# Filling the causal latent attention with projection products of later stages, and normalising one step ahead

## The reference, cut to what matters

```python
c_q = rms_norm(q_down, q_norm_g)                       # (512, 384)
q = (c_q @ w_uq).reshape(B, S, 8, 128 + 64)            # 8 heads
q_nope, q_rope = q[..., :128], apply_rope(q[..., 128:], cos, sin)
c_kv = rms_norm(kv_down, kv_norm_g)                    # (512, 256)
k_nope = (c_kv @ w_uk).reshape(B, S, 8, 128)
v = (c_kv @ w_uv).reshape(B, S, 8, 128)
# for each block i of 128 queries, each head h:
s = (q_nope @ k_nope.T + q_rope @ k_rope.T) * 192 ** -0.5
s = where(key <= query, s, -1e30)
o = softmax(s) @ v
```

## Time and profile before

| | |
|---|---|
| median of 3 runs | 1750.23 us (1749.51 to 1750.47) |
| the profiled execution | 1749.98 us, of which the span is 1748.1 us |
| PE busy | 1664.5 us, 95% |
| DVE, ACT, POOL busy | 859.7 us (49%), 580.7 us (33%), 536.2 us (31%) |
| mean granted PE clock | 0.978 of full |
| first scores of the first half | at 919.6 us |
| first half's last output done | at 962.25 us |
| second half's first scores | at 988.3 us |
| end of its last output, first `pool` tile begins | at 1030.8 us |
| third `pool` tile begins | at 1042.0 us |

### The profile page before, as it was taken

One profiled execution on the slowest core, in us unless ns is written; L12 is line 12 of the kernel. 1 busy time (PEld: TensorE's weight loads), 2 busy tenths in 40 slices (PEclk: granted clock), 3 DMA queues, 4 the chain that ended last, 5 costly groups with the idle time before them and its releaser, 6 DMA issues. The chain is left out here.

```text
span 1748.1 us, 20572 instructions
## 1 busy us (share of the span) xinstructions
PE 1664.5 (95%) x7732; PEld 1251.1 (72%) x7732; DVE 859.7 (49%) x1437; ACT 580.7 (33%) x956; POOL 536.2 (31%) x225
## 2 busy tenths in 40 slices
PE   6999889999999999999998899999999979999996
PEld 4878668887888888887775668888777855556553
DVE  4338476125644466335676854352334454334335
ACT  4117454334322244334424232342343231211113
POOL 3432126732344446732421214464324200000000
PEclk9999999999999999999999999999999989999998
DMA  4321113522322323521221112243313359888871
GB/s 163 97 84 49 61 62 121 168 85 67 95 89 94 97 86 124 165 85 37 85 73 37 60 49 92 92 143 98 95 48 97 152 182 371 331 341 337 334 289 49
DMA packets 50195, 226.51 MB, mean 130 GB/s; under 512 B 5952, under 2 KB 6848, under 8 KB 45504
## 3 DMA queue, kind: packets, MB, share of 16 engines
q1 hardware_dynamic: 48384, 220.50, 36.4%
q10 hardware_dynamic: 1728, 4.87, 0.8%
HBM read 223.25 MB, written 2.10 MB: 129 GB/s over the span
## 5 line engine op out<-in xcount | busy, mean ns | idle before, releaser
L488 POOL TENSOR_TENSOR lo_ring<-w_ring,hi_ring 128x1024 fp32r<-128x1024 f32 x219 | 535.7, 2447 | 852.3 <-ACT hi_ring L507 852.0
L507 ACT ACTIVATE hi_ring<-w_ring 128x1024 fp32r<-128x1024 f32 x219 | 231.4, 1059 | 657.0 <-PE G L1630 656.6
L1630 PE MATMUL G<-xa_hi,hi_ring 128*128 128x512 f32 x928 | 379.8, 409 | 19.5 <-POOL lo_ring L488 12.5
L1630 PE MATMUL G<-xa_hi,lo_ring 128*128 128x512 f32 x928 | 372.6, 402 | 0.0
L1630 PE MATMUL G<-xa_lo,hi_ring 128*128 128x512 f32 x928 | 370.0, 399 | 0.0
L1630 PEld LDWEIGHTS G<-xa_hi,hi_ring 128*128 128x128 f32 x928 | 176.8, 191 | 64.4 <-issue 14.1
L1630 PEld LDWEIGHTS G<-xa_lo,hi_ring 128*128 128x128 f32 x928 | 177.1, 191 | 44.6 <-issue 1.7
L1630 PEld LDWEIGHTS G<-xa_hi,lo_ring 128*128 128x128 f32 x928 | 176.7, 190 | 41.9
L1630 PE MATMUL G<-yb_hi,hi_ring 128*128 128x512 f32 x388 | 154.6, 398 | 0.0
L1630 PE MATMUL G<-yb_lo,hi_ring 128*128 128x512 f32 x388 | 151.8, 391 | 0.0
L1630 PE MATMUL G<-yb_hi,lo_ring 128*128 128x512 f32 x388 | 151.6, 391 | 0.0
(11 more groups left out here) (298 smaller groups left out, 2629.6 us busy)
## 6 DMA issues: line engine op xcount, KB each, us to landing
w_ring<-in_stream_dram SPq DMA_DIRECT2D x219, 512.0 KB, 3.6
arena<-in_w_gu_dram SPq DMA_DIRECT2D x16, 2048.0 KB, 8.1
ex_rings<-in_w_dn_dram SPq DMA_DIRECT2D x40, 512.0 KB, 13.6
ex_low<-in_w_gu_dram SPq DMA_DIRECT2D x8, 2048.0 KB, 12.5
ex_rings<-in_w_gu_dram SPq DMA_DIRECT2D x8, 2048.0 KB, 12.4
arena<-in_w_dn_dram SPq DMA_DIRECT2D x16, 512.0 KB, 11.5
sq<-in_w_dn_dram SPq DMA_DIRECT2D x8, 512.0 KB, 15.4
X<-in_x_in_dram SPq DMA_DIRECT2D x8, 256.0 KB, 6.2
```

What stands on the lines that cost most here:

```text
L488: nc.gpsimd.tensor_tensor(lo_ring[:, s, :], w_ring[:, s, :], hi_ring[:, s, :], ALU.subtract).then_inc(low, 1)
L507: nc.scalar.activation(hi_ring[:, m % RING, :], w_ring[:, m % RING, :], ACT.Copy).then_inc(high, 1)
L1630: return nc.tensor.matmul(*args, **kw)
```

## The change

In the first half, only `uv0`, `uk0` and `uq0` are made ahead of the steps. The products of `uv1` and `uk1` are cut into 16 pieces of three matmuls and PE does one piece in each step (two ahead of the first step, none in the last two). In the second half, the 16 pieces are those of the first two `pool` tiles. The pieces write banks 2 and 1 of `G` in turn, so the scores move from banks 2 and 3 to banks 3 and 0. The values and keys of the second half get places of their own, `vh1` and `kn1`, which lie over the parts of `yb_hi` and `yb_lo` that the same heads' outputs fill later. DVE takes the pieces' banks out in its odd steps (`beside`), normalises one step ahead, and scales `X` in the second half's steps. ACT rounds two of the next weight units after its first three exponentials and one more in step 10. PE's waits for the queries of steps 2 and 3 go up by one.

```diff
@@ -340,6 +340,8 @@
         vh = A(6016, 4, T)
         mP, mPT = A(8064, 2, T), A(9088, 4, T)
         qn, kn = U[:, 0:4, :], U[:, 4:8, :]
+        vh1 = ex_raw[:, 2:4, :].rearrange("p a b -> p (a b)").rearrange("p (h c) -> p h c", h=4)
+        kn1 = ex_low[:, 4 * T:KT * T].rearrange("p (h c) -> p h c", h=4)
         b_gl, b_gs, b_tmp = A(8064, 2, T), A(9088, 2, T), A(10112, T)
         pu, pa, pb_ = A(0, T + 16), A(528, T + 16), A(1056, T + 16)
         edge = A(1600, 4, 16)
@@ -387,7 +389,10 @@
             return u % 4
 
         def score(u, lo, hi):
-            first = ACC0["e_ag"] + u // TT if u < SU["x0"] else 3 if u >= SU["x2"] else 0
+            if u < SU["x0"]:
+                first = ACC0["e_ag"] + u // TT
+            else:
+                first = 3 if u >= SU["x2"] else 1 if u >= SU["mla"] else 0
             return S[:, at(u), lo:hi] if at(u) < 2 else G[:, (first + at(u)) % BANKS, lo:hi]
 
         def prob(probs, u, lo, hi):
@@ -404,6 +409,9 @@
 
         def x2_o(j):
             return (O[:, :], G[:, 0, :], TR[:, :], O[:, :])[j]
+
+        def beside_bank(n):
+            return 2 - n % 2
 
         block = ctx.enter_context(nc.Block())
 
@@ -701,29 +709,34 @@
                 unit_done("qd", j)
                 norm_tile("qd", j, U[:, j, :], V("q_norm", j), lat_hi[:, j, :], (evac, ACC0["qd"] + j + 1))
             base = SU["mla"]
+            unit_done("uv0", 0)
+            norm_root("qd", 384)
+            unit_done("uk0", 0)
             for half in range(2):
-                for name, k in ((f"uv{half}", 1), (f"uk{half}", 1), (f"uq{half}", 3)):
-                    for j in range(k):
-                        unit_done(name, j)
-                        if name == "uv0":
-                            norm_root("qd", 384)
+                unit_done(f"uq{half}", 0)
 
                 def one(u):
                     exps(base + u, 1, P * (u % TT + 1), 192 ** -0.5, mP)
 
                 for u in range(3):
                     one(16 * half + u)
+                for j in range(1, 3):
+                    unit_done(f"uq{half}", j)
                 for u in range(16 * half, 16 * half + 16):
                     t = u % TT
                     copy_t(base + u, mPT[:, 0:t + 1, t * P:(t + 1) * P], P * (t + 1), True)
                     if u + 3 < 16 * half + 16:
                         one(u + 3)
+                    if u % 16 == 10:
+                        unit_done("pool" if half else "uv1", 0)
                     if t == TT - 1:
                         j = u // TT
                         high_of((o_full, OB["mla"] + j + 1), O[:, :], yb_hi[:, j, :])
+                if half == 0:
+                    unit_done("uk1", 0)
             act.dma_start(edge, pool_edge).then_inc(edge_land, 16)
             act.dma_start(m2raw, mem2_in).then_inc(mem_land[2], 16)
-            for g in range(4):
+            for g in range(1, 4):
                 unit_done("pool", g)
             for f in range(KT):
                 if f == KT - 1:
@@ -1290,24 +1303,30 @@
                     scaled(ACC0["qd"] + j, U[:, j, :], RB[:, :])
                 norm_tile("qd", j, U[:, j, :], V("q_norm", j), lat_hi[:, j, :], lat_lo[:, j, :])
             base = SU["mla"]
+            for t in range(TT):
+                by_token(ACC0["uv0"] + t, vh[:, t, :], rck[:, t:t + 1])
+            norm_cols("qd", rcq)
+            for j in range(4):
+                scaled(ACC0["uk0"] + j, kn[:, j, :], RBk)
+            norm_bc("qd", RBq)
+            note(nc.vector.tensor_tensor(cosq, cos2, RBq, ALU.mult))
+            do(nc.vector.tensor_tensor(sinq, sin2, RBq, ALU.mult))
+
+            def beside(n):
+
+                a = ACC0["uv1"] + n
+                take(a)
+                bank = G[:, beside_bank(n), :]
+                if n < TT:
+                    nc.vector.tensor_scalar(vh1[:, :, n * P:(n + 1) * P], bank.rearrange("p (h d) -> p h d", h=4),
+                                            rck[:, n:n + 1], None, ALU.mult).then_inc(evac, 1)
+                else:
+                    nc.vector.tensor_tensor(kn1[:, n - TT, :], bank, RBk, ALU.mult).then_inc(evac, 1)
+
             for half in range(2):
                 if half:
 
                     dve.wait_ge(o_full, 24 + 4)
-                for t in range(TT):
-                    by_token(ACC0[f"uv{half}"] + t, vh[:, t, :], rck[:, t:t + 1])
-                if half == 0:
-                    norm_cols("qd", rcq)
-                for j in range(4):
-                    scaled(ACC0[f"uk{half}"] + j, kn[:, j, :], RBk)
-                    if half:
-                        for f in range(2 * j, 2 * j + 2):
-                            note(nc.vector.scalar_tensor_tensor(X[:, f, :], X[:, f, :], V("final1", f), RBf,
-                                                                ALU.mult, ALU.mult))
-                if half == 0:
-                    norm_bc("qd", RBq)
-                    note(nc.vector.tensor_tensor(cosq, cos2, RBq, ALU.mult))
-                    do(nc.vector.tensor_tensor(sinq, sin2, RBq, ALU.mult))
                 a = ACC0[f"uq{half}"]
                 for e in range(2):
                     rotated(a + 3 * e, cosq, sinq)
@@ -1324,13 +1343,22 @@
 
                 for u in range(3):
                     top(16 * half + u)
+                normalise(base + 16 * half, 1, P, mP)
                 for u in range(16 * half, 16 * half + 16):
-                    normalise(base + u, 1, P * (u % TT + 1), mP)
+                    if u + 1 < 16 * half + 16:
+                        normalise(base + u + 1, 1, P * ((u + 1) % TT + 1), mP)
                     if u + 3 < 16 * half + 16:
                         top(u + 3)
                     if u % TT == 1 and u > 16 * half + 1:
                         mla_low(u // TT - 1)
+                    if half == 0 and u % 2 == 1:
+                        beside(u // 2)
+                    if half and u % 16 in (0, 1, 3, 5, 7, 9, 11, 13):
+                        f = (u % 16 + 1) // 2
+                        note(nc.vector.scalar_tensor_tensor(X[:, f, :], X[:, f, :], V("final1", f), RBf,
+                                                            ALU.mult, ALU.mult))
                 mla_low(4 * half + 3)
+            settle()
             dve.wait_ge(edge_land, 16)
             for g in range(4):
                 a = ACC0["pool"] + g
@@ -1938,16 +1966,38 @@
                 tile("qd", j, xa_hi, xa_lo)
             base = SU["mla"]
             pe.wait_ge(rb_ready, NB["kvd"][0] + 1)
+            wide("uv0", 1, TT, lat_hi, lat_lo, 3, 2)
+            norm_cols("qd")
+            for j in range(4):
+                tile("uk0", 0, lat_hi, lat_lo, acc=ACC0["uk0"] + j, k0=3, k=2, part=j)
+            norm_bc("qd")
+
+            def beside(half, p):
+
+                if half:
+                    piece("pool", p // KT, xa_hi, xa_lo, [p % KT])
+                    return
+                t, kk = divmod(p, 2)
+                bank = G[:, beside_bank(t), :]
+                if kk == 0:
+                    pe.wait_ge(evac, ACC0["uv1"] + max(0, t - 1))
+                    unit_ready(UNIT0["uv1"] if t < TT else UNIT0["uk1"])
+                if t < TT:
+                    rows_of = slice(t * P, (t + 1) * P)
+                    ins = three(bank, UNIT0["uv1"], slice(kk * T, (kk + 1) * T), lat_hi[:, 3 + kk, rows_of],
+                                lat_lo[:, 3 + kk, rows_of], kk == 0, kk == 1, True)
+                else:
+                    b = 2 * (t - TT) + kk
+                    ins = three(bank, UNIT0["uk1"], slice(b * P, (b + 1) * P), lat_hi[:, 3 + kk, :],
+                                lat_lo[:, 3 + kk, :], kk == 0, kk == 1)
+                if kk == 1:
+                    ins.then_inc(full, 1)
+
             for half in range(2):
-                wide(f"uv{half}", 1, TT, lat_hi, lat_lo, 3, 2)
-                if half == 0:
-                    norm_cols("qd")
-                for j in range(4):
-                    tile(f"uk{half}", 0, lat_hi, lat_lo, acc=ACC0[f"uk{half}"] + j, k0=3, k=2, part=j)
-                if half == 0:
-                    norm_bc("qd")
                 for i, j in enumerate(UQ_ORDER):
                     a = ACC0[f"uq{half}"] + i
+                    if half and i == 1:
+                        pe.wait_ge(evac, a - 1)
                     bank_free(a)
                     for kk in range(3):
                         b = 3 * j + kk
@@ -1959,7 +2009,7 @@
 
                 def queries_ready(u):
                     if u % 16 in (0, 2, 3, 8, 12):
-                        pe.wait_ge(evac, ACC0[f"uq{half}"] + {0: 2, 2: 3, 3: 4, 8: 5, 12: 6}[u % 16])
+                        pe.wait_ge(evac, ACC0[f"uq{half}"] + {0: 2, 2: 4, 3: 5, 8: 5, 12: 6}[u % 16])
 
                 def scores(u):
                     h, t = divmod(u, TT)
@@ -1968,25 +2018,30 @@
                     queries_ready(u)
                     scores_free(base + u)
                     s = score(base + u, 0, w)
```

(13 more changed lines are left out.)

## The result

The changed kernel takes 1731.53 us (median of 4 runs, 1730.54 to 1738.98) where the kernel before takes 1750.35 (4 runs): a ratio of 0.989, with a 95% interval of 0.9868 to 0.9913, 18.8 us less. The profiled execution took 1731.94 us, its span 1730.1: 18.04 us less than the profiled execution of before.

The account below looks back on a forecast made before the run. PE, busy 95%, bounds the kernel, so only its waits and low clock can be won. Gains 8.1 + 1.9 + 5.4 = 15.4, less 1.7, give 13.7: 1749.98 to 1736.3, median about 1736.5 us; range 1731.8 to 1743.1.

Parts of the forecast that it names:

- The ceiling and the pieces: In the changed stretch: at most 26.2 us to win; pieces take 0.70 each, and switching costs nothing.
- First half, queries, second half: The changed stretch's three parts: gains of 8.1, 1.9 and 5.4 us, with both tails at full clock.
- The clock in the tails: Ends of both halves: one tail of two falls to the low clock, its output costing 1.7 us more.
- All else unchanged: Outside the changed stretch: no clock change counted; PE reaching `br_mla` 11.3 us sooner was put at nothing.
- 13.7: Whole program: forecast gain in us, 15.4 less 1.7 for one fallen tail; chance 0.53.
- The rule of the Trainium skill: Both tails: cycling through PSUM banks with small idle times can lose the clock; neither tail safe, gain 12.0 us.
- DVE late in the loops: Rival, both halves: POOL's splits stall DVE three more times by 2.2 us; gain 7.1, 1743.1 us; chance 0.10.
- Given back behind the loops: Rival, fifth `br_mla` tile: late `pool` chains hold PE 4 us; gain 9.7, 1740.5 us; chance 0.07.
- The wait for banks: Rival, first half's even pieces: PE waits for DVE to empty banks; slower, 1760 us at 3 us each; chance 0.04.
- The better end of case 3: Rival, tails and second half: neither clock falls, DVE slips before POOL; gain 17.6, 1732.6 us; both-ends chance 0.22.
- the 0.3: Fourth scores of a half: 0.3 us more, since DVE gives back their bank later.
- the 0.4: Second half's start: taking out queries meets POOL's splitting, some 0.4 us more before the first transpose.

Follow-up runs that it names:

- shifts: Four or eight overwritten matmuls added between the attention and its next tile: changed kernel 1735.2 and 1733.8 us, kernel before 1750.7 and 1753.8.
- the banks alone: Kernel before with only the score banks changed (3 and 0 for 2 and 3) and the query waits of steps 2 and 3 one higher: 1750.02 us.
- `normalise` alone: Kernel before with only normalising moved one step ahead: 1745.19 us, ratio 0.9969.
- the run with the pieces moved out: Changed kernel with the last two pieces of each half made in step 11, leaving the tails empty: 1742.33 us, ratio 0.9956.

## Why the prediction was wrong

By its own steps, between the two profiled executions:

- *The ceiling and the pieces.* Right. 26.2 us were given as the most to win in the stretch; 16.6 were won. Switching between pieces and steps costs nothing: 10.38 for a middle head forecast at 10.4.
- *First half, queries, second half.* 45.8, 12.9 and 48.4 were forecast; 45.4, 12.7 and 47.9 measured. The waits came as named: 1.4 forecast on the first copy of each half, 0.99 and 0.98 measured; nothing on the queries; 2.2 and 2.22 on `normalise`. Together the sum was 1.2 us too dear: 0.4 in each half for that copy, and 0.4 for queries that were to meet POOL in the second half, which did not come (the first transposes follow the first scores by 6.25 us in the first half and 6.26 in the second); the rest evens out.
- *The clock in the tails.* The one step of the written sum that failed in its mechanism: "I take one fallen tail of the two". Both kept the clock: 1.7 us. The case against it, that the last 2.6 us of a tail hold transposes only, as before, did not hold: 19 tails with pieces kept the clock.
- *All else unchanged.* The largest miss, and it was not even written as a step: the sum was made as if the clock elsewhere stayed, a term put at nothing without a reason. The program took 2.5 us less behind the stretch, with 6.8 us less of low clock there, and 1.0 more ahead of it. With 13.7 + 1.7 + 1.2 + 2.5 - 1.0 this gives 18.1, where 18.04 were measured between the profiles. The medians add 0.8 to it.
- *The rule of the Trainium skill* (TensorE: Matmul & The Clock Gate, "A second HAM failure mode: psum-queue depth-cycling") would have cost another 1.7. The runs with pieces speak against it here: the middle heads and the tails with pieces cycle through banks and are at clock 1.00. The 11 of 13 tails without pieces that lost the clock would agree with it.
- *The rivals.* DVE late in the loops: 8.04 of 10.3 busy, no wait of PE on it in a middle head; POOL did hold `normalise` for 2.23 us in the first half too, and PE did not wait for it. Given back behind the loops: PE has no idle time there for 219 us. The wait for banks: none in the loop; 0.24 ahead of the fourth scores, as forecast (0.3). The better end of case 3, no fallen tail, was the right one in its clock, though `X` did meet POOL.
- *The range.* Its lower end, 1731.8, had room for one fallen tail less, for 2.2 us at `X` that were not won, and for 0.8 of costs put too high (the 0.3, once in each half, and the 0.4 make 1.0), none for the clock outside the stretch. One stretch of low clock more or less is worth 1.3 us, and one or two of them came or went behind the stretch in most of the kernels here.
- *The parts of the change.* The order of `normalise` was costed at nothing. Alone it wins 5.5 us in the medians (4.3 in the stretch); taken out of the changed kernel it costs 7.7 (3.0 in the stretch). All the rest without it still wins 10.9. That hidden part of the 13.7 I had put down to the pieces. The sum itself did not need the split, so this did not move the number.

What stays open: whether the 2.5 us behind the stretch belong to the change. The changed kernel had 703.5, 703.9, 706.4 and 705.0 by shifts of 0, 0, 1.0 and 1.9 us; the kernel before 706.0, 706.6 and 707.6. With the banks alone and with `normalise` alone it had 704.7. The shifts show that the moment matters, not that the averages over all moments are equal. And ahead of the stretch, where PE has the same instructions in all 16 profiles, single executions took 917.3 to 923.9 us, with 20.5 to 27.3 us of low clock: a difference of 1 or 2 us between two profiles can come without any change at all. So on which side of the range's end the time fell is in part chance: the 2.9 us of kept tails and of costs put too high have a cause that the traces show, the 2.5 behind do not.

## What to carry to other kernels

Where an engine-bound program has a chain that passes through several engines, independent matmuls cut into pieces of 0.7 us cost nothing between its steps here; put them first where the chain has no work of its own ahead, its start and its tail, since there they also kept the clock. When a filling is added, look at once at what the other queues now do at the start of each loop (here two weight units split in one go, beside two DVE operations from SBUF): rounding them apart and scaling `X` later made the stretch 4.7 us shorter (101.2 for 105.9). And when a change moves a wait of PE, widen the range by the low clock elsewhere: 1.3 us for each stretch that may come or go.

## What the runs showed of the hardware

- The low clock came in stretches of 3.4 us, alone or one after the other (6.8, 10.2, 13.7, 17.1), in all 16 profiles; only the last one, at the end of the program, is 14.4 to 16.3 us long. A stretch inside a busy part of the program cost 1.3 us: what lies behind the third `pool` tile took 703.5 to 703.9 us with 17.1 us of low clock in it (4 profiles), 704.7 to 705.6 with 20.5 (5), 706.0 to 706.6 with 23.9 (5) and 707.6 with 27.3 (1).
- The same wait of PE lost the clock or kept it by when it came: 1.0 us of added work turned the later attention from clock 1.00 to 0.91, one empty tail of two kept it in the run with the pieces moved out, and the wait of 2.22 was followed by low clock in that run and not in the changed kernel.
- Such patterns can repeat from one execution to another: the two profiles of the changed kernel have the same eight low stretches at the same places to within 1 us. They need not: ahead of 915 us, in the same instructions, the banks-alone run has none near 195, and the run with `normalise` alone has 6.8 us from 881 to 888 where the kernel before has 3.4 from 874 to 877.
- In the changed kernel a DVE operation from SBUF that began beside one of POOL's splits ended 0.2 to 0.6 us after it (the scaling of `X` took 2.75 us for 0.74); one that reads a PSUM bank took its usual 0.74 beside POOL.
